# An expert stage with three named experts, nine slabs loaded ahead, and the gate applied after the gathering

## The reference, cut to what matters

```python
def hier_moe(h, lw):
    gp = softmax(t @ moe_w_rg + moe_b_rg)          # 4 groups, the best one is taken
    ...                                            # in it the best 2 of 4 experts
    gate = one_hot(group) * (g_w * within)         # 16 experts, 2 of them nonzero for each token
    a = einsum("nd,edf->nef", t, lw["moe_w1"])
    b = einsum("nd,edf->nef", t, lw["moe_w3"])
    y = einsum("nef,efd->nd", silu(a) * b * gate[..., None], lw["moe_w2"])
...
x = x + g2 * hier_moe(modulate(rms_norm(x, norm2_g), sh2, sc2), lw)
```

## Time and profile before

| | us |
|---|---|
| three runs, lowest, median, highest | 1231.79, 1234.66, 1242.47 |
| the profiled execution, its own time | 1233.34 |
| its span, as the trace shows it | 1231.4 |
| expert stage of layer 0, first product of batch 0 to the end of Y(8) | 392.6 to 628.0 |
| the same of layer 1 | 979.5 to 1215.9 |
| PE busy | 1099.9 (89% of the span) |
| DVE busy | 560.3 (45%) |
| ACT busy | 290.8 (24%) |
| POOL busy | 94.4 (8%) |

### The profile page before, as it was taken

The page is one execution under the profiler, slowest core; times in us unless marked ns, Lnnn a source line. Parts: engine busy times, 40 slices in busy tenths (PEclk is TensorE's granted clock), DMA queues, the critical chain, the costliest instruction groups (busy, mean ns, idle before and its releaser), DMA issues.

```text
span 1231.4 us, 18736 instructions
## 1 busy us (share of the span) xinstructions
PE 1099.9 (89%) x7505; PEld 539.0 (44%) x7505; DVE 560.3 (45%) x1436; ACT 290.8 (24%) x717; POOL 94.4 (8%) x112
## 2 busy tenths in 40 slices
PE   4899999698998999987689999987999999997776
PEld 1455544365456333322235655445755733332222
DVE  1257887457248321111262679856744742111124
ACT  0247412233113111000011682232332311100000
POOL 0020001310001000000011000040000100000001
PEclk9899999799999999999989999988999999999988
DMA  8570133886954999999993203356495499999996
GB/s 357 200 194 1 69 94 114 233 327 232 387 200 184 414 423 420 420 422 422 419 363 114 82 1 94 137 132 251 156 377 225 156 414 423 420 420 422 420 422 262
DMA packets 90794, 333.29 MB, mean 271 GB/s; under 512 B 29631, under 2 KB 32071, under 8 KB 59975
## 3 DMA queue, kind: packets, MB, share of 16 engines
q1 hardware_dynamic: 80999, 299.66, 62.5%
q0 software_dynamic: 7392, 23.93, 5.7%
q10 hardware_dynamic: 2304, 8.39, 1.7%
HBM read 314.38 MB, written 17.56 MB: 270 GB/s over the span
## 4 chain that ended last, share of the span: by engine, by line
PE 70%; SPq 10%; DMA 9%; DVE 5%; issue 3%; ACT 2%; DVEq 0%; ACTq 0%
PE bank L576 66%; SPq L1313 10%; DMA arena<-in_moe_w_dram 4%; PE bank L579 4%; DMA ring<-in_w_in_dram 2%; ACT arena L1492 2%; DMA ring<-in_ada_w_dram 1%; DVE x L1822 1%; DMA ring<-in_w_out_dram 1%; DVE ring L1822 1%; DVE x L1814 1%; DVE arena L1814 1%; DVE small L1822 0%; DVE small L2136 0%; SPq L1402 0%
## 5 line engine op out<-in xcount | busy, mean ns | idle before, releaser
L576 PE MATMUL bank<-ring,arena 128*32 128x512 f32 (+1 forms) x2272 | 331.7, 587 | 30.2 <-issue 16.0
L576 PE MATMUL bank<-arena 128*32 128x512 f32 (+3 forms) x1600 | 270.5, 567 | 18.7 <-DMA arena<-in_moe_w_dram 11.0
L1492 ACT ACTIVATE arena<-bank 128x512 f32<-128x512 f32 (+3 forms) x302 | 129.0, 473 | 584.2 <-PE bank L579 400.0
L576 PE MATMUL bank<-ring,hT 128*128 128x512 f32 x576 | 258.2, 604 | 7.8 <-DMA ring<-in_w_in_dram 4.2
L576 PEld LDWEIGHTS bank<-ring,arena 128*32 128x32 f32 (+1 forms) x2272 | 99.3, 114 | 220.7 <-issue 218.3
L576 PEld LDWEIGHTS bank<-ring,hT 128*128 128x128 f32 x576 | 109.6, 194 | 136.7 <-issue 129.6
L1814 DVE TENSOR_TENSOR arena<-bank,mrow 128x512 f32<-128x512 f32 x36 | 24.9, 692 | 229.2 <-PE bank L576 229.2
L576 PE MATMUL bank<-hT,ring 128*128 128x384 f32 x384 | 128.2, 488 | 0.1
L576 PEld LDWEIGHTS bank<-arena 128*32 128x32 f32 (+2 forms) x1600 | 81.5, 124 | 96.7 <-issue 82.4
L576 PEld LDWEIGHTS bank<-hT,ring 128*128 128x128 f32 x384 | 71.2, 190 | 46.9 <-issue 1.3
L579 PE MATMUL bank<-const,arena 128*128 128x128 f32 x443 | 67.1, 287 | 19.5 <-DMA x<-in_x_prompt_dram 8.6
(11 more groups left out here) (157 smaller groups left out, 846.2 us busy)
## 6 DMA issues: line engine op xcount, KB each, us to landing
ring<-in_moe_w_dram SPq DMA_DIRECT2D x120, 1024.0 KB, 20.7
arena<-in_moe_w_dram SPq DMA_DIRECT2D x72, 1024.0 KB, 19.5
ring<-in_ada_w_dram SPq DMA_DIRECT2D x24, 2048.0 KB, 8.8
ring<-in_w_in_dram SPq DMA_DIRECT2D x14, 2048.0 KB, 9.1
ring<-in_w_out_dram SPq DMA_DIRECT2D x4, 2048.0 KB, 9.4
expert_dram<-arena ACTq DMA_DIRECT2D x16, 512.0 KB, 8.3
tok_dram<-arena POOLq DMA_DIRECT2D x6, 512.0 KB, 2.9
arena<-in_na_rpb_dram SPq DMA_DIRECT2D x16, 96.0 KB, 7.0
```

Source lines behind the costliest of these rows:

```text
L576: return nc.tensor.matmul(out, lhsT, rhs, start=start, stop=stop)
L1492: return nc.scalar.activation(out, in_, func, **kw)
```

## The change

Three experts are named, so that nine slabs (three experts with three matrices) are known before routing, and a ninth slot (slot 8, in `arena`) is made by moving the small buffers: the fetched results `y_e`, the turned tokens `xT_e` and the selection matrices now lie on other tiles. All nine are loaded before routing; no slot is left for a ranked expert's slab until A(0) has given one back. Position 3, the first ranked one, goes to the expert with the fewest tokens (`fewest`, `spot`), and positions 4 to 7 have three strips. There are still 48 slabs, 36 strips and 9 batches.

Only eight slabs are still loaded in halves: the four after the nine, and w3 and w2 of the last batch's two experts. All others are one DMA of 2 MB, issued when the whole phase before has been done, and a phase waits for the whole slab.

The first tokens are picked by tiles: tiles 0 and 1 after `places_of(0, 2)`, half of the columns before and half after the placing of tile 2, then tile 2. The router's exponents are taken after the first selection. Results leave PSUM by a plain copy, and g2 is multiplied after the gathering, in `other_rows`, which has four operations a tile; only batch 8, which is not gathered, is still multiplied by `row_gate`. The transposes and copies that make g2 into rows stand in the last batch (`gate_halves`, `gate_kept_rows`).

The diff, cut to its core:

```diff
+MOE_SLOTS = [8, 1, 2, 5, 4, 0, 6, 7, 3]
+FREED = [0, 1, 2, 5, 6, 7, 8, 4, 3]
+SPARE_SLOTS = [1, 2, 5, 4, 0, 6]
+GATE_SLOT = 8
...
+NAMED, WIDE = 3, 4
 RANKED = EXPERTS - NAMED
-STRIPS = [UNITS if NAMED <= p < NAMED + WIDE else UNITS - 1 for p in range(EXPERTS)]
...
+                given_back.append((slab, (what, n)))
+    slots = len(MOE_SLOTS)
+    early = [slab for slab in needed if slab[0] < NAMED][:slots]
+    needed = early + [slab for slab in needed if slab not in early]
+    place, loads = {}, []
+    for i, slab in enumerate(needed):
+        old, phase = given_back[i - slots] if i >= slots else (None, None)
+        place[slab] = i if i < slots else place[old]
+        loads.append((slab, phase))
+    in_halves = needed[slots:slots + QUAD] + [(p, m) for p in sorted(set(holders(BATCHES - 1))) for m in (1, 2)]
+    turn, held = [{}, {}], [[0] * slots, [0] * slots]
+    for slab in needed:
+        for half in range(2 if slab in in_halves else 1):
+            held[half][place[slab]] += 1
+            turn[half][slab] = held[half][place[slab]]
     return phases, loads, place, turn, held
...
+                            for t in tiles:
+                                last = mm(bank[(3, 7)[half]][:, q * P:(q + 1) * P], tok_sb[:, t, k * P:(k + 1) * P],
+                                          sel_first[:, t, 0:P], (q, t) == (0, 0), (q, t) == (3, TILES - 1))
+                        if tiles[-1] == TILES - 1:
+                            last.then_inc(es["transposed"], 1)
+                b = dve_bank("place", l, 0)
...
+                places(b[:, 16:32], 1).then_inc(for_dve, 1)
+                token_rows(2)
+                pe.wait_ge(act_emptied, job["tok", l, 1, 1])
+                pe.wait_ge(ada_taken, jobs["ada"] // SHARE)
+                pe.wait_ge(es["first_sel"], 2 * l + 1)
+                first_tokens((0, 1), (0,))
+                b = dve_bank("place", l, 2)
+                pe.wait_ge(routed, TILES * l + 3)
+                places(b[:, 0:16], 2)
+                for s in range(TILES):
+                    last = mm(b[:, 16:32], ones, chosen[:, s, :], s == 0, s == TILES - 1)
                 last.then_inc(for_dve, 1)
-                b = dve_bank("count", l)
-                for s in range(TILES):
-                    last = mm(b[:, 0:16], ones, chosen[:, s, :], s == 0, s == TILES - 1)
-                last.then_inc(for_dve, 1)
+                first_tokens((0, 1), (1,))
...
                         second_product(end - 1)
+                        pe.wait_ge(gate_kept, 4 * (l + 1))
                         h_cols(end - 1)
...
                         if n > first:
                             results(n - 1)
+                        if n == end - 1:
+                            gate_halves((3,))
                         if n < end - 1:
                             second_product(n)
                         if n == first:
...
+                def gate_halves(which):
+                    pe.wait_ge(late_in, l + 1)
+                    for i in which:
+                        s, half = divmod(i, 2)
+                        for q in range(4):
+                            last = tr(bank[(0, 1, 5, 4)[i]][:, q * P:(q + 1) * P],
+                                      mods[:, l, 5 * KC + 4 * half + q, s:s + 1].broadcast_to([P, P]))
+                        last.then_inc(gate_full, 1)
...
+                first_tokens((2,))
+                list_of(es, 4 * l, LIST_UNITS[0])
...
+                    p, m = slab
+                    if len(held_by) == NAMED and p >= NAMED:
+                        sp.wait_ge(ranked, l + 1)
                     if p not in held_by:
...
-                waited = False
+                    put(MOE_SLOTS[i], m, held_by[p] + l * EXPERTS, moe_in[half or 0][i], half)
...
+                        freed = [slab for slab, at in LOADS if at == phase and (half or slab in TURN[1])]
...
+                        for slab in freed:
+                            load(slab, half if slab in TURN[1] else None)
...
                 token_rows(2)
-                gate_rows(l, 2, (1,))
                 act.wait_ge(router_x, l + 1)
                 f(r_exp, r_exp, ACT.Exp).then_inc(router_e, 1)
...
+                def gate_kept_rows(i):
+                    act.wait_ge(gate_full, 4 * l + i + 1)
+                    s, half = divmod(i, 2)
+                    f(gate2[:, s, half * 512:(half + 1) * 512], bank[(0, 1, 5, 4)[i]][:]).then_inc(gate_kept, 1)
...
                 dve.wait_ge(y_in[t], 32 * (l + 1))
-                link(stt(x[:, t, :], y_first[:, t, :], w_tok[:, t, 0:1], x[:, t, :], ALU.mult, ALU.add))
-                ins = stt(x[:, t, :], y_second[:, t, :], w_tok[:, t, 1:2], x[:, t, :], ALU.mult, ALU.add)
+                both = y_first[:, t, :]
+                link(ts(both, both, w_kept[:, t, 0:1]))
+                link(stt(both, y_second[:, t, :], w_kept[:, t, 1:2], both, ALU.mult, ALU.add))
+                link(tt(both, both, gate2[:, STREAM[t], :]))
...
+                def places_of(t0, t1, source, last):
+                    many = t1 - t0
+                    b = filled(*source)
+                    stt(place[:, t0:t1], b[:, 0:16 * many].rearrange("p (t n) -> p t n", t=many), 1.0, chosen[:, t0:t1],
+                        ALU.add, ALU.mult).then_inc(dve_emptied if last else dve_step, 1)
+                    if last:
+                        dve.wait_ge(dve_emptied, job[source])
+                    else:
+                        dve.wait_ge(dve_step, n(dve_step))
+                    link(ts(shifted[:, t0:t1], place[:, t0:t1], -1.0, op0=ALU.add))
+                    for t in range(t0, t1):
+                        ins = tt(sel_first[:, t, :].rearrange("p (e n) -> p e n", e=2), heads(tab("slot")[:, 0:LEAST], 2),
+                                 over(shifted[:, t, 0:2], LEAST), ALU.is_equal)
+                    ins.then_inc(es["first_sel"], 1)
+                places_of(0, 2, ("place", l, 0), True)
                 best_experts(2)
-                tt(r_exp[:, :, 0:4], lg[:, :, 0:4], over(m_g, 4), ALU.subtract)
...
+                    link(ts(fewest, rank, float(RANKED - 1), op0=ALU.is_ge))
+                    link(stt(spot, fewest, -float(RANKED), rank, ALU.mult, ALU.add))
+                    link(ts(spot, spot, 1.0, op0=ALU.add))
...
+                def last_row_gates():
+                    dve.wait_ge(gate_kept, 4 * (l + 1))
+                    at = BATCHES - 1
+                    link(ts(row_gate, gate2[:, 1, :], flags[:, 1, at:at + 1]))
+                    link(stt(row_gate, gate2[:, 0, :], flags[:, 0, at:at + 1], row_gate, ALU.mult, ALU.add))
...
+                dve.wait_ge(dve_emptied, job["place", l, 2])
                 count()
                 owners()
                 ranks()
                 select(es, 0, True)
+                tt(r_exp[:, :, 0:4], lg[:, :, 0:4], over(m_g, 4), ALU.subtract)
+                tt(r_exp[:, :, 4], m_2, m_1, ALU.subtract).then_inc(router_x, 1)
...
```

More of the change, by code:

```diff
@@ new lines, in first_tokens @@
+                def first_tokens(tiles, halves=(0, 1)):
+                    for half in halves:
+                        for q in range(4):
+                            k = 4 * half + q
+                            for t in tiles:
[3 more added lines that the diff above has]
+                            last.then_inc(es["transposed"], 1)
@@ L1422, in _ @@
                         slab_done([name for name in PRE[l] if pre_slot[name] == s][-1])
-                    for piece in pieces:
-                        load(piece)
+                    load(LOADS[MOE_SLOTS.index(s)][0])
                 for phase in PHASES:
@@ L1428, in _ @@
                     for half in range(2):
-                        freed = [piece for piece, at in LOADS[2 * len(MOE_SLOTS):] if at == (what, n_, half)]
+                        freed = [slab for slab, at in LOADS if at == phase and (half or slab in TURN[1])]
                         m_ = n_ + l * BATCHES + 1
@@ L1777, in _ @@
                         tokens_T(es, n_ + 1, (n_ + 1 - first) % 2, n_ < 1)
+                    if n_ == end - 1:
+                        for i in range(3):
+                            gate_kept_rows(i)
                     if n_ > first:
```

293 lines of the change are left out of this document (107 added, 186 removed).

## The result

| | before | after |
|---|---|---|
| median (lowest to highest, 4 runs each), us | 1234.29 (1231.79 to 1242.47) | 1250.38 (1248.31 to 1253.15) |
| profiled execution, its span, us | 1233.34, 1231.4 | 1250.82, 1248.7 |
| granted clock of TensorE over the span | 0.964 | 0.944 |

The changed kernel takes 1.0114 of the time of before (95% interval 1.0082 to 1.0145), 14 us more by this ratio; the two medians lie 16 us apart, the two profiled spans 17.3. Forecast were 10 more, 1244 us in a range of 1230 to 1251. The measured median lies 0.6 us inside the upper end of that range.

A forecast was written before the change was run, and what follows sets the result against it. The weight stream sets when late batches run, then PE's own chain sets the end. Expert stages -0.6, layer change +4.1 and end +6.0 gave +9.5 on 1233.34, 1242.8; with the median 1.3 higher, 1244 us, range 1230 to 1251.

The forecast's parts named there:

- Row sums, +10.1 forecast: `other_rows` on DVE: four operations for two, +2.0 us a tile; +4.1 at the layer change, +6.0 at the program's end.
- Late restart: Weight stream after routing: all slots full, first load only 3.7 us after A(0)'s start, 396.75 against 388.45, +8.3 us.
- five fewer pieces: Weight stream: Y(7)'s last weight is complete with piece 71 after routing instead of 76, -12.5 us a layer.
- my middle value of 1.9 us: Weight stream: 16 KB rows of whole slabs save 3.9 us a layer or nothing; the middle, -1.9, was taken.
- +3.5 for whole slabs: Expert stage, Y(7): both halves, instead of one, stand behind the last slab's arrival, +3.5 us a layer.
- The clock penalty of 1.7: PE in Y(7): some 3 us of idle time ahead lowers its clock; between 0 and +1.7 us, +1.7 taken.
- Work that waits for no weight: Expert stage behind Y(7)'s last wait: the branch, B(8) and Y(8) need no weight; 22.5 us, which stays.
- Routing, +0.5 a layer: From last selection to A(0): small added operations on the router's path start A(0) at 393.05, half a microsecond later.
- The mixing stage, nothing forecast: Stretch from w_ba to tile 2's norm product in layer 1, untouched by the change: difference 0 forecast.
- 2 (the stream runs dry): Early batches: batch 2's gather lands late, PE loses 7.5 us, +4 us a layer, 1248 us; chance 20%.
- 1: Rival, shorter stage: router's chain does not grow, 16 KB rows gain 2.5%, Y(7) keeps its clock; 1232 us, chance 17%.
- 4: Rival, something larger, as two layers' three slabs loaded ahead counting in full; 1215 us, chance 5%.

The follow-up runs named there:

- experiment 2: Kernel before with the changed kernel's four row-sum operations in `other_rows`, nothing else; ratio 1.0083 to the kernel before, 10.3 us.
- experiment 1: Changed kernel with `other_rows` back at two operations on x, so batches 0 to 7 get no g2; ratio 1.0013 to the kernel before.
- experiment 6: Changed kernel with w2 of position 13, Y(7)'s last slab, in halves and w1 of position 5 whole; ratio 1.0106 to the kernel before.
- 11: Changed kernel with PE's branches exchanged, w2 of position 13 in halves and last layer's tile 0 row sum ahead of batch 8's result; 1.0010, 1239.7 against 1238.0 us.
- Experiment 4: Changed kernel with placing of tile 2 and the counts ahead of the first half of the first tokens in PE's queue; ratio 1.0092 to the kernel before.
- 5: Changed kernel with 24 unread transposes in PE's idle time at the layer change, ahead of layer 1's first norm product; ratio 1.0061 to the kernel before.
- 10: Changed kernel with PE's two branches exchanged, common case first; ratio 1.0038 to the kernel before, 9 us less than the changed kernel.
- 3: Changed kernel with eight unread transposes of g2 put back ahead of tile 2's norm product, both layers; ratio 1.0132 to the kernel before.
- 9: Kernel before with PE's two branches exchanged, common case first; ratio 0.9973 to the kernel before.
- 7: Kernel before with the last layer's tile 0 row sum ahead of batch 8's result; ratio 0.9984, not told apart from 1.
- 12: Kernel before with PE's branches exchanged, early tile 0 row sum, and each next tile's row sum ahead of the previous direct product; 0.9960, 1234.3 against 1240.4 us.

## Why the prediction was right in its number, and where its steps were not

The number was met with luck in it: 1250.4 is 6 us above the point forecast, 0.6 below the end of the range, and two costs that the forecast did not have were in part made up by a stage that gained more than forecast.

- **Row sums, +10.1 forecast: right.** 10.3 us by the ratio of experiment 2, 10.1 by the stretches of experiment 1. They are some 70% of the surplus.
- **The stream: right in its parts.** Late restart, five fewer pieces and the faster stream gave Y(7)'s last weight at 596.2; my terms (-12.5 + 8.3 - 1.9 from 601.84) say 595.7. The faster rows gave about 1% over the whole stage, which is what my middle value of 1.9 us comes to. The first load was off: it went out 6.4 us behind A(0)'s start in layer 0 and 4.5 in layer 1, not 3.7 (the granted clock was 0.79 from 392 to 400), so 2.1 us later than forecast in layer 0. What made up for it is, as far as the rates show, that the late restart cost less than its time: before, the stream was not at full rate when it began, 193 GB/s from 388 to 392 and 403 from 392 to 400.
- **Y(7), +3.5 for whole slabs: confirmed in layer 1** by experiment 6 (3.3 us back), and not in layer 0 (1.0 back). The two runs with the halves (6 and 11) took 208.1 and 208.0 us from A(0) to Y(7) in layer 1, the six without 210.9 to 213.0; in layer 0 they took 209.8 and 209.9 against 210.0 to 212.3. The clock penalty of 1.7 did not come: I expected 3 us of idle time ahead of Y(7), it was 1.48 in layer 0 and 0.41 in layer 1. From A(0) to Y(7) the stage is shorter by 2.2 and 2.6 us in the pair, by 2.3 and 0.8 when five runs with the changed kernel's loads as they were (1, 4, 5, 10 and the kernel itself) are set against six with those of before; with 3 among them it is 2.5 and 0.7.
- **"Work that waits for no weight" behind Y(7): wrong,** though it cost no accuracy here. It held only because PE lost 4 us at its branch. Without the jump the kernel before waits for weights in B(8) in both layers (9); the changed one does not in 10, and does again in layer 1 of 11, where Y(7) ends earlier. The lead of the changed stream is to be read there: B(8)'s last weight let PE go 221 us behind A(0) in 9 and 215 in layer 1 of 11. Behind the jump neither kernel could use it.
- **Routing, +0.5 a layer: the term that was mis-sized.** I priced operations at full clock and left out what filled PE's time before. On average over six profiles with the program of before and seven with the changed one (3 left out) routing took 19.4 and 20.0 us (layers 0 and 1) before and 20.9 and 21.9 after: +1.5 and +1.9. The +5.1 of the profiled pair sets one of the two shortest of before (17.88) against one of the longest after (23.00). Routing of layer 1 follows the granted clock in both programs: before, 17.9 us at 0.90 and 22.1 at 0.69; after, 19.0 at 0.99 (3), 20.4 at 0.92 (5 and 6) and 23.0 at 0.66. The 1.89 us ahead of the norm product are part of it and not all: of 14 norm products behind such a gap ten took 3.3 to 3.8 us and four 2.05, while all 14 behind a gap of 1.0 took 2.05. Experiment 4 shows that the order in the queue is not the cause in layer 1. What else sets the clock in this stretch stays open.
- **The mixing stage, nothing forecast: +4.5.** The step that failed is that work which the change does not touch costs the same. All seven runs with the changed PE program and nothing or little moved in it (the changed kernel, 1, 4, 6, 10, 11, and 3) stop once among these 48 products, for 1.4 to 2.3 us; none of the six with the program of before does, nor does 5. In 1, 4 and 10 the stop comes after the same 33 products, in 3, which has eight more products ahead of it, after 26, in 6 and 11 after 34. The place in PE's program decides, not the work. The stop is a wait for the next piece of code: in all seven the transfer of a packet of q8 begins while PE is in these short products, and PE goes on 1.3 to 1.5 us after its end; in the other seven profiles it begins in one of the groups of 16 products of 512 columns beside them, and PE does not stop. Only in the changed kernel and in 1 did the 16 products behind run at half clock, so the stop is 3 us of the 4.5 there and 1.4 to 2.3 elsewhere. And 7, without the stop, took 298.7 us as well: the stage has other causes of 2 to 3 us that are not found.
- **Rivals.** 2 (the stream runs dry) did not occur: the gather landed as forecast and the share never fell. Of 1, neither half came: the stream gained 1% over the stage, not 2.5% for the whole slabs, and the router's chain grew; only the clock of Y(7) was as it says. 4 did not come either. What made the time longer than forecast was in none of them.

Summed over runs rather than over one pair: rows +10.2, routing +3.4, A(0) to Y(7) -3.1, mixing stage of layer 1 +3.2 (299.2 us on average over the seven with the stop, 296.0 over the six of before) give +13.7, beside 14 by the ratio and 16 by the medians. The sum leaves out the stretch from Y(7) to batch 8's result, whose spread is larger than any difference in it.

## What to carry to other kernels

A gap that waits for nothing can hide a wait behind it: before counting on the idle chain behind the last wait, ask what would stop it if the gap were gone. Price code that is taken out of an engine's idle time too, since the engine may come out of the longer gap at half its clock, and code that is only moved along in the engine's program. When a gap is named issue, look in the DMA view for what landed at its end: here it was a slab ahead of A(8), and a packet of code at the jump and in the mixing stage. And put the rare case behind the common one, so that the jump falls where the engine waits anyway.

## What the runs showed of the hardware

- With rows of 16 KB the stream moved 423 to 425 GB/s, with rows of 8 KB 418 to 421. The Trainium skill (DMA: Bandwidth & Descriptors, Specifications) gives some 358 GB/s as the HBM limit of one core, half of a stack's 716. The expert stages, run by one core, are above it, and the measurement decides.
- PE's jump over the rare case cost 3.4 to 4.4 us of idle time (ten profiles, two layers), and none when the common case came first (9 to 12). The idle time ended 1.7 to 1.8 us after a packet of q8 had been moved.
- In layer 1's mixing stage PE stopped for 1.4 to 2.3 us where the transfer of such a packet began in 48 products of 64 x 64 (1.6 us for all; seven profiles), and did not stop where it began in 16 products of 512 columns (1.9 to 3.6 us; the other seven).
- Code is loaded while the kernel runs; the page of the changed kernel has a queue for it:

```profile
q8 instruction: 64, 1.05, 0.3%
```

  The Trainium skill (Trainium Architecture — The Big Picture, The software stack) has the runtime move the instruction streams into the engines at load. That can't be all: 64 packets of 16 KB are moved on this queue in the profile of one execution.
- The same PE program took from 22.5 to 28.4 us from Y(7) to batch 8's result (runs of before, 2 and 7), by gaps named issue and half clock behind them. Single profiles of this kernel differ by more than the effects of 1 to 3 us that one would like to read from them. What sets this from run to run stays open.
